# Attention stage of a hybrid encoder layer: scores written to SBUF together with their minimum, exponentials from SBUF, two transpose banks, a deeper pipeline

## The reference, cut to what matters

```
s = einsum('bnqd,bnkd->bnqk', qblk, kt).astype(f32) * scale
p = softmax(s, axis=-1).reshape(B, H, 2, Q_BLOCK, T)
p = p[:, :, 0] - lam * p[:, :, 1]
return einsum('bhqk,bhkd->bhqd', p.astype(vt.dtype), vt)
```

## Time and profile before

| | us |
|---|---|
| median of 3 runs | 2922.42 |
| lowest and highest run | 2915.84, 2923.0 |
| span of the profiled execution, first to last instruction | 2916.6 |
| the attention stage in it, first scores to last output | 1170.9 to 1578.5 |
| TensorE busy in the whole span | 2812.6 (96%) |

### The profile page before, as it was taken

One profiled execution on the slowest core, in us unless ns is written; L12 is line 12 of the kernel. 1 busy time (PEld: TensorE's weight loads), 2 busy tenths in 40 slices (PEclk: granted clock), 3 DMA queues, 4 the chain that ended last, 5 costly groups with the idle time before them and its releaser, 6 DMA issues. The chain is left out here.

```text
span 2916.6 us, 44672 instructions
## 1 busy us (share of the span) xinstructions
PE 2812.6 (96%) x18476; PEld 1754.8 (60%) x18476; DVE 1377.3 (47%) x2307; ACT 981.8 (34%) x1676; POOL 631.4 (22%) x377
## 2 busy tenths in 40 slices
PE   8899999999999999899999999988999999999999
PEld 6566666666666666677777887764444444444443
DVE  3555464656565554677776655555431111112513
ACT  3323242333323232566565677572300000000001
POOL 1132231314041312100000134250143333330000
PEclk9999999999999999999999999998999999999999
DMA  3142433424242535234410567864411111113012
GB/s 97 63 154 86 161 121 119 153 80 159 95 159 74 173 97 163 68 92 98 120 34 10 139 157 176 192 200 135 136 50 48 47 44 44 44 43 130 0 36 87
DMA packets 192505, 297.73 MB, mean 102 GB/s; under 512 B 84480, under 2 KB 119072, under 8 KB 186032
## 3 DMA queue, kind: packets, MB, share of 16 engines
q1 hardware_dynamic: 181936, 252.20, 29.6%
q10 hardware_dynamic: 10368, 42.67, 3.6%
HBM read 188.54 MB, written 106.27 MB: 101 GB/s over the span
## 5 line engine op out<-in xcount | busy, mean ns | idle before, releaser
L641 PE MATMUL pp_ps<-uT,pp_w 128*128 128x347 f32 x3072 | 904.8, 455 | 3.8 <-PEq L190 2.5
L641 PEld LDWEIGHTS pp_ps<-uT,pp_w 128*128 128x128 f32 x3072 | 579.4, 189 | 318.7 <-issue 6.1
L1462 DVE TENSOR_REDUCE at_mn<-at_S 128x1 f32<-128x1040 f32 x128 | 156.2, 1239 | 41.8 <-PE at_S L1283 40.8
L1283 PE MATMUL at_S<-at_kR,at_qR 64*128 64x512 f32 (+1 forms) x768 | 162.1, 499 | 13.5 <-ACT at_v L1385 5.6
L866 POOL TENSOR_TENSOR pp_neighbours<-pp_raw 128x1040 f32<-128x1040 f32 x24 | 46.0, 1919 | 591.8 <-ACT pp_raw L742 591.8
L1352 PE MATMUL at_ob<-at_v,at_pT 128*128 128x128 f32 x1152 | 162.2, 286 | 0.5
L2321 PE MATMUL fh_b<-u2T,fh_ws 128*128 128x512 f32 x352 | 158.2, 592 | 0.0
L2321 PE MATMUL fh_b<-fh_t,fh_ws 128*128 128x512 f32 x352 | 154.7, 592 | 0.0
L1352 PEld LDWEIGHTS at_ob<-at_v,at_pT 128*128 128x128 f32 x1152 | 138.2, 191 | 17.1 <-DVE at_o L1469 15.4
L1408 ACT ACTIVATE at_p<-at_S,at_mn 128x1040 f32<-128x1040 f32 x128 | 144.6, 1130 | 8.6 <-DVE at_mn L1462 8.0
L1283 PEld LDWEIGHTS at_S<-at_kR,at_qR 64*128 64x128 f32 x768 | 89.9, 189 | 94.8 <-issue 68.5
(11 more groups left out here) (292 smaller groups left out, 4536.3 us busy)
## 6 DMA issues: line engine op xcount, KB each, us to landing
pp_w<-in_w_main SPq DMA_DIRECT2D x64, 512.0 KB, 3.8
s_kept<-pp_ob ACTq DMA_DIRECT2D x48, 520.0 KB, 4.9
fh_w<-in_w_ffn_in SPq DMA_DIRECT2D x44, 512.0 KB, 4.5
rc_kb<-s_kb SPq DMA_DIRECT2D x64, 256.0 KB, 3.8
rc_aw<-s_ar SPq DMA_DIRECT2D x64, 256.0 KB, 4.1
s_ar<-pp_ar SPq DMA_DIRECT2D x8, 1088.0 KB, 4.0
s_kb<-pp_kb SPq DMA_DIRECT2D x8, 1088.0 KB, 7.2
s_vz<-pp_vz SPq DMA_DIRECT2D x8, 1088.0 KB, 9.0
```

What stands on the lines that cost most here:

```text
L641: ins = nc.tensor.matmul(ps[s][:, n, 0:NW], weights, moving[:, n * NW:(n + 1) * NW], start=(k == 0), stop=(k == len(parts) - 1))
L1283: return nc.tensor.matmul(S[m][:, c:c + w], qR[h % 2][rows, q0:q0 + P], kR[h % 2][rows, c:c + w], start=True, stop=True)
L1462: nc.vector.tensor_reduce(mn[t % 2][:, m:m + 1], S[m][:, 0:T], AX, ALU.min).then_inc(least[m], 1)
```

## The change

Scores and minimum. `find_least` becomes `keep_scores`: a DVE `tensor_scalar` that multiplies a map by 1.0, takes the smaller of it and 3.0e38, writes the 1040 results to SBUF (`pr`) and gives their minimum by its accumulator output. Both passes of a step start only when both maps are scored. The exponentials then read and write `pr` in place. The next step's scores wait for the two DVE passes (`least`) and no longer for the exponentials (`raised`).

PSUM. The two maps of scores share five banks: map 0 from column 0, map 1 from column 1520, so that the third bank holds the last 16 columns of map 0 and the first 16 of map 1. All six pieces are issued in one run, the 16 columns of map 0 first and those of map 1 last. The bank that comes free is a second transpose bank: `tb` is now two tiles, one for each group of 4 blocks.

The last block. `pr` has 1040 columns (before 1152 for map 0). GpSimd copies the last 16 columns of the combined map to a small tile `rest` with zeros behind them, once per step; TensorE transposes `rest` into place 0 of the first transpose bank (`turn_rest`), ACT copies it (`keep_rest`). The transposes of v use places 1 and 2 of that bank, in steps 3 to 7 of a head.

Order. `pr`, `sums`, `inv` and `coef` have three copies (`HELD_P`). TensorE's pass t is now: scores(t), turn_rest(t-3), turn_values, all nine values(t-3), turn(t-2) of both groups. ACT's: exponential of map 1 of t-1, copies of t-3 (two groups and the rest), keep_values, exponential of map 0 of t. DVE's: combine(t-2), scale_output(t-4), both keep_scores(t). SP stores the output of t-4 in pass t. The loops run 3 or 4 passes beyond the last step instead of 2.

The core of the diff:

```diff
-SCORES = [(c, min(512, T - c)) for c in range(0, T, 512)]
-GROUPS = [(0, 4), (4, 8), (8, 9)]
+MAP_AT = (0, 3 * BANK - META)
+SCORES = [(0, SEQ, META), (1, META, BANK), (0, 0, BANK), (1, META + BANK, BANK), (0, BANK, BANK), (1, 0, META)]
+LAST_OF = ((0, BANK), (1, 0))
+GROUPS = [(0, 4), (4, 8)]
+HELD_P = 3
...
-        S = [ctx.enter_context(nc.psum_tensor(f"at_S{m}", [P, 3 * 512], F32)) for m in range(2)]
-        beside = S[1][:, 2 * 512 + P:3 * 512].rearrange("p (b k) -> p b k", k=P)
-        tb = ctx.enter_context(nc.psum_tensor("at_tb", [P, 4, P], F32))
+        S = ctx.enter_context(nc.psum_tensor("at_S", [P, 5 * BANK], F32))
+        tb = [ctx.enter_context(nc.psum_tensor(f"at_tb{j}", [P, 4, P], F32)) for j in range(2)]
...
+                for t in range(STEPS):
+                    pool.wait_ge(combined, done(t))
+                    if t >= 2:
+                        pool.wait_ge(rest_turned, done(t - 2))
+                    nc.gpsimd.tensor_copy(rest[t % 2][:, 0:META], pr[t % HELD_P][0][:, SEQ:T]).then_inc(rest_kept, 1)
...
                     if t > 0:
                         for m in range(2):
-                            pe.wait_ge(raised[m], done(t - 1))
+                            pe.wait_ge(least[m], done(t - 1))
+                    for m, c, w in SCORES:
+                        rows, at = slice(DQ * m, DQ * m + DQ), MAP_AT[m] + c
+                        if (m, c) == (1, 0):
+                            pe.wait_ge(meta_scored, done(t))
+                        ins = nc.tensor.matmul(S[:, at:at + w], qR[h % 2][rows, q0:q0 + P], kR[h % 2][rows, c:c + w],
+                                               start=True, stop=True, skip_group_check=True)
...
+                def turn_rest(t):
+                    pe.wait_ge(rest_kept, done(t))
+                    pe.wait_ge(copied, group_done(t, 0))
+                    nc.tensor.transpose(tb[0][:, 0, :], rest[t % 2][:], ident[:]).then_inc(rest_turned, 1)
...
+                for t in range(STEPS + 3):
                     if t < STEPS:
                         scores(t)
+                    if t >= 3:
+                        turn_rest(t - 3)
+                    if t < STEPS and values_at(t):
+                        turn_values(*values_at(t))
+                    if t >= 3:
+                        values(t - 3)
+                    if 2 <= t < STEPS + 2:
+                        for j in range(NG):
+                            turn(t - 2, j)
...
-                    nc.scalar.activation(pr[t % 2][m][:, 0:T], S[m][:, 0:T], ACT.Exp, bias=mn[t % 2][:, m:m + 1], scale=-1.0,
-                                         accum_out=sums[t % 2][:, m:m + 1]).then_inc(raised[m], 1)
+                    nc.scalar.activation(scores[:], scores[:], ACT.Exp, bias=mn[t % 2][:, m:m + 1], scale=-1.0,
+                                         accum_out=sums[t % HELD_P][:, m:m + 1]).then_inc(raised[m], 1)
...
-                    nc.vector.tensor_reduce(mn[t % 2][:, m:m + 1], S[m][:, 0:T], AX, ALU.min).then_inc(least[m], 1)
+                    nc.vector.tensor_scalar(pr[t % HELD_P][m][:], map_of(m), 1.0, FAR, ALU.mult, ALU.min,
+                                            accum_out=mn[t % 2][:, m:m + 1]).then_inc(least[m], 1)
```

More of the change, by code:

```diff
@@ L1195, in attention @@
         v_turned, v_kept, tails_cleared = sem("at_v_turned"), sem("at_v_kept"), sem("at_tails_cleared")
-        scored = [sem(f"at_scored{m}") for m in range(2)]
+        scored, meta_scored = [sem(f"at_scored{m}") for m in range(2)], sem("at_meta_scored")
         least = [sem(f"at_least{m}") for m in range(2)]
@@ L1240, in _ @@
                 load_v(1)
-                for t in range(STEPS + 2):
-                    if t >= 2:
-                        store(t - 2)
+                for t in range(STEPS + 4):
+                    if t >= 4:
+                        store(t - 4)
+                    if t >= STEPS:
+                        continue
                     if t >= NQ and t % NQ == 2:
@@ L1263, in _ @@
                 last = slice(SLOTS, SLOTS + 1)
-                for tile in (vT, pr[0][0], pr[1][0]):
-                    nc.gpsimd.memset(tile[:, T:TPAD], 0.0).then_inc(tails_cleared, 1)
+                nc.gpsimd.memset(vT[:, T:TPAD], 0.0).then_inc(tails_cleared, 1)
+                for s in range(2):
+                    nc.gpsimd.memset(rest[s][:, META:P], 0.0).then_inc(tails_cleared, 1)
                 pool.wait_ge(tails_cleared, 3)
@@ L1279, in _, with scores @@
             def _(pe):
-                def score(t, m, c, w):
+                def scores(t):
                     h, q0 = t // NQ, QB[t % NQ]
[L1282 to L1286, removed]
                     if t % NQ == 0:
-                        h = t // NQ
                         if h == 0:
@@ L1352, in values @@
+                def values(t):
+                    h = t // NQ
+                    if t > 0:
+                        pe.wait_ge(o_scaled, done(t - 1))
+                    if t % NQ == 0:
+                        pe.wait_ge(v_kept, NV * h + NV)
+                    for b in range(NBLK):
+                        if b == 4:
+                            pe.wait_ge(copied, group_done(t, 1))
+                        if b == NBLK - 1:
+                            pe.wait_ge(rest_copied, done(t))
                         ins = nc.tensor.matmul(ob[:, 0:P], pT[t % 2][:, b, :], v[h % 2][:, b, :],
@@ L1397, in keep_turned @@
                     b0, b1 = GROUPS[j]
[L1398 to L1406 removed]
+                    nc.scalar.copy(pT[t % 2][:, b0:b1, :], tb[j][:]).then_inc(copied, 1)
@@ L1425, in _ @@
                     if t == 0:
                         keep_first_values()
+                    if t >= 3:
+                        for j in range(NG):
+                            keep_turned(t - 3, j)
+                        keep_rest(t - 3)
+                    if t < STEPS and values_at(t):
+                        keep_values(*values_at(t))
+                    if t < STEPS:
+                        raise_scores(t, 0)
             @block.vector
@@ L1454, in combine, with keep_scores @@
                                                    ALU.add).then_inc(combined, 1)
-                def find_least(t, m):
-                    dve.wait_ge(scored[m], done(t))
+                def keep_scores(t, m):
+                    if m == 0:
+                        for n in range(2):
+                            dve.wait_ge(scored[n], done(t))
+                        if t >= HELD_P:
+                            dve.wait_ge(turned, group_done(t - HELD_P, NG - 1))
+                            dve.wait_ge(rest_kept, done(t - HELD_P))
```

160 lines of the change are left out of this document (64 added, 96 removed).

## The result

The changed kernel takes 2871.77 us, the median of four runs (2869.04 to 2876.28), the kernel before 2919.13 in the same comparison. The ratio is 0.9846, 95% interval 0.9831 to 0.9861: 45 us faster, 41 to 49. Forecast were 38.3 us less, 2884.1, in a range of 2870 to 2904; the measured time lies in it, 1.8 us above its lower end.

What follows compares the result with a forecast made beforehand. TensorE's own work, 5.635 us a step against 6.225, was taken as the new bound: 35.4 us saved over 60 steps, plus 3.3 at the beginning, minus 0.4 at the end, 38.3 off 2922.4, giving 2884.1 us; range 2870 to 2904.

Steps and rivals of the forecast that it cites:

- (c): TensorE's own work in a step, taken as the new bound: 5.635 us, lower ends 5.43, upper ends 5.83.
- R3: Rival: TensorE is truly full at 98% and keeps its pace whatever waits go; no gain, 2920 us, chance 0.05.
- (a): Scores no longer wait for exponentials; DVE's new pass takes 1.30 us, the ring 5.05, or 5.35 with a separate read-out.
- (d): Possible TensorE stalls in the new order: reordering costs nothing, with 0.3 us of slack at ACT's tightest place.
- (g): SP's queue: outputs stored two passes later, same stores and loads, room in the order; costs nothing.
- (h): Beginning of the stage: scores(3) start near 1189 instead of 1192.29, gain 3.3 us; 1.6 less if scores(2) meet a low clock.
- (i): End of the stage, from scores(63) to the last scaling's end: 13.1 us against 12.7, a loss of 0.4.
- R1: Rival: late waits or dearer DVE passes; the ring or ACT's order sets steps of 5.85 to 6.05 us; 2903, chance 0.14.
- R2: Rival: DVE's pass with running minimum goes at half rate, 2.3 us; ring 7.05 us a step, 2974 us, chance 0.09.
- the ring: Chain closing each step: before, scores, two minima, one exponential, 6.45 us with turned values; new, scores and two DVE passes, 5.05.

Runs made afterwards that it cites:

- Experiment 5: Changed kernel without the ninth value product, 2862.91 us; with one more DVE pass a step, 2878.22 us; with each map read twice by DVE, 2991.93 us.
- x_wait_exp: Changed kernel, but the scores wait for both exponentials of the step before again: 2924.40 us, ratio 1.0029 to the kernel before.
- experiment 4: Changed kernel, but the last 16 columns of map 1 are scored apart, after the rest's transpose and turned values: 2902.22 us, ratio 0.9945 to the kernel before.
- Experiment 2: Kernel before, with only DVE's pass writing scores to SBUF and the scores waiting for that pass; old order, banks and depth: 2926.60 us, ratio 1.0036.
- x_two_passes: Changed kernel, but DVE reads each map twice, a reduction for the minimum and a plain pass to SBUF: 2991.93 us, ratio 1.0270 to the kernel before.
- x_one_bank: Changed kernel, but both groups of four transposes go through the first transpose bank: 2996.13 us, ratio 1.0278 to the kernel before.

## Why the prediction was right, and where it was off

**The bound (c, R3).** Right: TensorE's own work sets the new step. Experiment 5 shows it from both sides. R3 (TensorE was full before) is out: in `x_wait_exp` TensorE has no more work than in the changed kernel, waits 0.7 to 0.9 us in every step, and the step is as long as before the change, so the wait and not the work set it.

**The sum.**

| term, us | forecast | measured |
|---|---|---|
| scores, one run | 2.20 | 2.14 |
| the rest's transpose | 0.16 | 0.16 |
| eighteen passes of values | 2.18 | 2.01 |
| eight transposes and return | 0.98 | 0.97 |
| turned values, average | 0.115 | 0.11 |
| waits, average | 0 | 0.055 |
| step, average | 5.635 | 5.449 |
| 60 steps | -35.4 | -46.6 |
| beginning | -3.3 | -1.7 |
| end | +0.4 | +3.9 |
| stage | -38.3 | -44.4 |

The average step is (1513.29 - 1186.38) / 60. "Beginning" is the time from the first scores to scores(3), "end" the time from scores(63) to the last output. The term that was mis-sized is the values, "1.21 for ten is 0.121 each". The 1.21 held the way out of the half-array form once, 0.10 by experiment 4, and the 0.97 for eight loads runs from the first start to the last end, which is seven starts and one duration of 0.19. The distance between starts is 0.111. By starts alone, as the prediction itself had set out to read, eighteen take 2.00. The scores in one run were the second such term, 2.14 instead of 2.20. The sum had given the added pair 0.18, with 0.14 as its least; by experiment 4 it costs 0.01. The other 0.11 over the old 2.02 is in the ten passes themselves, which take 2.13 in that experiment, now that a 16-column piece goes first; that this order is the cause was not tried.

Some figures of the prediction do not come out of its own numbers. The lower ends of (c) add up to 2.16 + 0.16 + 2.18 + 0.88 + 0 + 0.115 = 5.495 us, not 5.43, which makes its fast end 2876 instead of 2872; the measured step of 5.449 is below it. The ring of 5.35 in (a) is 5.33 with 1.24 + 0.20 a pass. And the 0.26 us of the turned values explains only part of the 0.48 between 6.45 and 5.97: passes that nothing holds start 1.15 us apart and not 1.24, and the scores came 1.36 instead of 1.47 us behind the start of the last exponential.

That the total came within 0.5% owes something to luck. The steps were 11.2 us shorter than forecast in all; the beginning and the end took 5.1 of that back. Within the steps, too, the waits that (d) and (g) put at nothing hid 3.3 us of the mistake in the values.

**The waits (d, g).** "I cost the reordering at nothing" held for ACT: none of its copies stops TensorE in a steady step. It missed DVE's wait for stores: "order there has room" was read from SP's sum of waits, and a sum says nothing of the three places where 14 loads lie between two stores. The store was slow before, too: in the first such place of the kernel before it was issued at 1288.22, 3.6 us after its scaling, and two such stores landed after 7.3 us in the median, but DVE asked for the tile only at 1297.16. The faster step brought that need forward. Cost 3.3 us.

**The beginning (h).** The case "if the clock is still low for scores(2), 1.6 less" came true:

```profile
1179.86 3.82 PE L1316 MATMUL at_S<-at_kR,at_qR 64*128 64x16 f32 x12 [2.73 <-DVE at_p L1478]
...
1186.38 2.17 PE L1316 MATMUL at_S<-at_kR,at_qR 64*128 64x16 f32 x12 [1.68 <-DVE at_p L1478]
```

The granted clock was 0.56 while scores(2) ran (1179.86 to 1183.70). In the kernel before they started at 1185.87 and took 2.08 us, at a granted clock of 1.00. There TensorE had the transposes and values of step 0 to do between scores(1) and scores(2); in the new order it has nothing between them and stands still for 2.73 us.

**The end (i).** This step failed, by 3.5 us: "copies to 10.7, the rest's turn and copy 11.1, values from 10.3". The last rows of the stage:

```profile
1522.17 1.04 PE L1350 MATMUL at_tb<-ident,at_p 128*128 128x128 f32 x8
...
1523.72 2.17 PE L1369 MATMUL at_ob<-at_v,at_pT 128*128 128x128 f32 x18
...
1525.73 1.04 PE L1350 MATMUL at_tb<-ident,at_p 128*128 128x128 f32 x8
...
1527.29 2.17 PE L1369 MATMUL at_ob<-at_v,at_pT 128*128 128x128 f32 x18
...
1529.51 0.35 DVE L1485 TENSOR_SCALAR at_o<-at_ob,at_inv 128x128 f32<-128x128 f32 x1 [3.22 <-PE at_ob L1369]
```

I had followed the data of step 63 and not TensorE's list. The data came in time: combine(63) ended 8.6 us after scores(63) started, forecast was 8.9. But in TensorE's list the transposes of step 63 stand behind the values of step 62, which wait for their own transposes and copy: each of the last steps costs 3.56 us in series. So the transposes of step 63 began at 12.4 us and not at 8.9, which is the whole miss; from there to the last scaling's end it took 4.1 us, forecast 4.2. A pipeline one step deeper leaves one more such round for the end.

**DVE's pass (a, R1, R2).** It takes 1.24 us, as the reduction did, so R2 fell. The read-out is a second instruction of 0.083 us, and passes start 1.16 us apart with it. The Trainium skill, VectorE: DVE Perf Modes, "Two Vector instructions with no wait between them", by which an op that writes out its accumulator is two instructions, agrees with the DVE_READ_ACCUMULATOR rows; the cost of the second is hidden in that distance. R2's price was right as a mechanism: at two passes a map the ring gave 7.14 us, forecast 7.05 for a pass of 2.3. R1 fell with it: the passes stay far under its 1.59 us, and ACT holds TensorE in no steady step.

**What the prediction did not see.** It credited the gain to the ring that the release opens. Experiment 2 shows that the old order had a second ring just behind the first, over `ob`, the scaling and the values, which came into force as soon as the first was opened. In the new order the scaling comes ahead of DVE's passes, and the values that it scales are ready long before; that this alone takes the second ring away is argued, since three copies of `pr` came with it.

## What to carry to other kernels

When a wait is taken out of a ring, walk each engine's list once around the next longest ring before counting the gain; here both the release and the order were needed, and each alone was worth nothing. Take TensorE's cost from distances between starts, and never divide a stretch that holds a change of array form or a first load's duration. For the end of a pipeline count what is left in each engine's list after the last input, not only the last item's own chain.

## What the runs showed that was not expected

- A bound on another engine can also cost clock: in `x_two_passes` TensorE, busy 40.5 of 50 us, was granted 0.93 on average, and a run of scores went from 2.18 to between 2.7 and 3.9 us in seven steps. In `x_one_bank`, where TensorE waits 1.85 us a step for ACT, five steps have such slow scores.
- The last pair of 16-column passes costs 0.01 us beside another map's 512 columns, and 0.52 a step when it stands apart between full-array work.
- GpSimd's copy of 16 columns took 0.20 us in this stage, where the copy of 17 columns took 0.72 beside busy DVE.
